# A float32 transformer block on one core: two weight splits moved ahead in the entries, gate and up by turns in the first chunk

## What is computed

```python
def swiglu(x, w_gate, w_up, w_down):
    return (jax.nn.silu(x @ w_gate) * (x @ w_up)) @ w_down
...
        h = layer_norm(DEEPNORM_ALPHA * h + 0.5 * swiglu(h, ffn1_w_gate[l], ffn1_w_up[l], ffn1_w_down[l]),
                       ln1_g[l], ln1_b[l])
        mix = hybrid_mixer(h, w_in[l], q_norm_g[l], kv_norm_g[l], w_uq[l], w_uk[l], w_uv[l], w_q_idx[l],
                           k_idx_ln_g[l], k_idx_ln_b[l], conv_w[l], a_log[l], dt_bias[l], o_norm_g[l], w_out[l])
        h = layer_norm(DEEPNORM_ALPHA * h + mix, ln2_g[l], ln2_b[l])
        h = layer_norm(DEEPNORM_ALPHA * h + 0.5 * swiglu(h, ffn2_w_gate[l], ffn2_w_up[l], ffn2_w_down[l]),
                       ln3_g[l], ln3_b[l])
```

## Time and profile before

| | us |
|---|---|
| median of 3 runs (lowest, highest) | 1978.47 (1975.74, 1982.19) |
| the profiled execution: its own time | 1978.86 |
| its span, first to last instruction | 1977.0 |
| mean granted TensorE clock over it | 0.995 of full speed |

### The profile page before, as it was taken

One profiled execution on the slowest core, in us unless ns is written; L12 is line 12 of the kernel. 1 busy time (PEld: TensorE's weight loads), 2 busy tenths in 40 slices (PEclk: granted clock), 3 DMA queues, 4 the chain that ended last, 5 costly groups with the idle time before them and its releaser, 6 DMA issues.

```text
span 1977.0 us, 28705 instructions
## 1 busy us (share of the span) xinstructions
PE 1948.3 (99%) x10670; PEld 1661.4 (84%) x10670; DVE 1091.0 (55%) x1235; ACT 845.2 (43%) x944; POOL 65.7 (3%) x95
## 2 busy tenths in 40 slices
PE   9999999999999998999999999899999999999997
PEld 7888888888888887999999988788888888888886
DVE  5555545555445465677756757555545555544455
ACT  4444434444434343555645544344444444443332
POOL 0000000000000001300221100000000000000000
PEclk9999999999999999999999999999999999999999
DMA  8666665666566573755532057466666666556663
GB/s 293 190 189 190 191 182 179 190 200 210 190 204 203 193 244 95 223 180 148 142 98 87 22 186 261 131 189 190 189 182 183 193 197 190 186 169 194 208 197 144
DMA packets 185327, 357.30 MB, mean 181 GB/s; under 512 B 11296, under 2 KB 23584, under 8 KB 184240
## 3 DMA queue, kind: packets, MB, share of 16 engines
q1 hardware_dynamic: 183568, 347.43, 56.8%
q0 software_dynamic: 1696, 8.99, 1.4%
HBM read 354.28 MB, written 2.10 MB: 180 GB/s over the span
## 4 chain that ended last, share of the span: by engine, by line
PE 95%; DVE 3%; issue 1%; ACT 1%; DMA 0%; SPq 0%; POOL 0%; POOLq 0%; ACTq 0%; DVEq 0%
PE acc L370 27%; PE acc L372 27%; PE acc L371 27%; PE acc L393 3%; PE acc L397 3%; PE acc L395 3%; PE tp L727 1%; DVE wlo L358 1%; PE acc L1946 1%; PE tp L1959 0%; ACT whi L351 0%; PE acc L1972 0%; PE tp L448 0%; DMA raw<-in_ffn_w_gate_dram 0%; DVE work L1691 0%
## 5 line engine op out<-in xcount | busy, mean ns | idle before, releaser
L358 DVE TENSOR_TENSOR wlo<-raw,whi 128x1024 fp32r<-128x1024 f32 (+2 forms) x637 | 762.4, 1204 | 785.5 <-ACT whi L351 784.6
L351 ACT ACTIVATE whi<-raw 128x1024 fp32r<-128x1024 f32 (+2 forms) x637 | 656.2, 1039 | 943.4 <-PE acc L372 880.8
L370 PE MATMUL acc<-whi,xT 128*128 128x512 f32 (+2 forms) x1652 | 636.3, 385 | 13.6 <-DVE wlo L358 12.8
L372 PE MATMUL acc<-whi,xT 128*128 128x512 f32 (+2 forms) x1652 | 631.3, 382 | 0.0
L371 PE MATMUL acc<-wlo,xT 128*128 128x512 f32 (+2 forms) x1652 | 630.8, 382 | 0.0
L370 PEld LDWEIGHTS acc<-whi,xT 128*128 128x128 f32 x1652 | 311.6, 189 | 79.4 <-DVE wlo L358 12.8
L372 PEld LDWEIGHTS acc<-whi,xT 128*128 128x128 f32 x1652 | 311.6, 189 | 59.8
L371 PEld LDWEIGHTS acc<-wlo,xT 128*128 128x128 f32 x1652 | 311.8, 189 | 56.7
L370 PE MATMUL acc<-whi,hT 128*128 128x512 f32 x656 | 256.3, 391 | 0.0
L372 PE MATMUL acc<-whi,hT 128*128 128x512 f32 x656 | 255.4, 389 | 0.0
L371 PE MATMUL acc<-wlo,hT 128*128 128x512 f32 x656 | 255.4, 389 | 0.0
(11 more groups left out here) (299 smaller groups left out, 1283.7 us busy)
## 6 DMA issues: line engine op xcount, KB each, us to landing
raw<-in_ffn_w_up_dram SPq DMA_DIRECT2D x176, 512.0 KB, 3.7
raw<-in_ffn_w_down_dram SPq DMA_DIRECT2D x176, 512.0 KB, 4.6
raw<-in_ffn_w_gate_dram SPq DMA_DIRECT2D x175, 512.0 KB, 3.8
raw<-in_w_in_dram SPq DMA_DIRECT2D x48, 512.0 KB, 3.8
raw<-in_w_out_dram SPq DMA_DIRECT2D x32, 512.0 KB, 6.6
raw<-in_w_in_dram SPq DMA_DIRECT2D x32, 260.0 KB, 2.8
raw<-in_w_in_dram SPq DMA_DIRECT2D x16, 456.0 KB, 5.3
raw<-in_w_q_idx_dram SPq DMA_DIRECT2D x8, 512.0 KB, 4.2
```

The lines of the kernel that those rows point to most:

```text
L351: act.activation(hi[:, s, :, 0:w], raw[:, r, :, 0:w], ACT.Copy).then_inc(hi_done, 1)
L358: dve.tensor_tensor(lo[:, s, :, 0:w], raw[:, r, :, 0:w], hi[:, s, :, 0:w].bitcast(F32), ALU.subtract).then_inc(lo_done, 1)
L370: pe.matmul(o, hi, w_hi[:, s, k, 0:width], start=first and k == 0, stop=False)
L372: ins = pe.matmul(o, lo, w_hi[:, s, k, 0:width], start=False, stop=last and k == UNIT_KT - 1)
```

## The change

In both entries ACT makes the high parts of units 9 and 10 before the turns of (2, 1) and (3, 0); DVE normalises (3, 1) and splits unit 9 before its turn of (2, 1), and splits unit 10 before its turn of (3, 0); PE does the transposes of (3, 0) ahead of unit 8 and those of (3, 1) ahead of unit 9. In the first chunk of the first FFN the stream's order is gate 0, up 0, gate 1, up 1, then gate 2 to 7 and up 2 to 7 (`FIRST`); the transfers of x come behind units 1, 3, 5 and 7 (`FIRST_X`); ACT and DVE split unit 1 ahead of x tiles 2 and 3; the tanh of gate comes behind split 11 instead of 9.

```diff
--- before.py
+++ after.py
@@ -421,12 +421,20 @@
 
 
 
-        def entry_pe(pe, u):
-
-            if u == 0:
-                pe.wait_ge(sem("xT_lo_first"), 1)
-            else:
-                pe.wait_ge(sem("xT_lo"), u // 2 + 1)
+        FIRST = [(0, 0), (1, 0), (0, 1), (1, 1)] + [(c, k) for c in range(2) for k in range(2, KU)]
+        FIRST_X = {1: 0, 3: 1, 5: 2, 7: 3}
+
+        def first_units_pe(pe):
+
+            for v, (c, k) in enumerate(FIRST):
+                if v == 0:
+                    pe.wait_ge(sem("xT_lo_first"), 1)
+                    first_unit_mm(pe)
+                else:
+                    if k > 0:
+                        pe.wait_ge(sem("xT_lo"), k // 2 + 1)
+                    unit_mm(pe, F1GU, 0, v, (acc0, acc1)[c], (acc0_free, acc1_free)[c], 0, "w", xT, 2 * k, k == 0,
+                            k == KU - 1, acc0a_done if c == 0 else None)
 
 
         def quarter_of(e, q, t):
@@ -497,13 +505,11 @@
             half_unit(6, 1)
             tile_to_xT_pe(pe, e, 2, 1)
             half_unit(7, 1)
+            tile_to_xT_pe(pe, e, 3, 0)
             for half in range(2):
                 half_unit(8, half)
-            tile_to_xT_pe(pe, e, 3, 0)
-            for half in range(2):
-                half_unit(9, half)
             tile_to_xT_pe(pe, e, 3, 1)
-            for v in range(10, 2 * KU):
+            for v in range(9, 2 * KU):
                 for half in range(2):
                     half_unit(v, half)
 
@@ -522,11 +528,11 @@
             split_hi(act, p, 0, 7)
             tile_to_xT_act(act, e, 2, 0)
             split_hi(act, p, 0, 8)
+            split_hi(act, p, 0, 9)
             tile_to_xT_act(act, e, 2, 1)
+            split_hi(act, p, 0, 10)
             tile_to_xT_act(act, e, 3, 0)
-            split_hi(act, p, 0, 9)
             tile_to_xT_act(act, e, 3, 1)
-            split_hi(act, p, 0, 10)
 
         def entry_splits_dve(dve, e, p):
 
@@ -542,12 +548,12 @@
             tile_to_xT_dve(dve, e, 2, 0)
             norm_tile(dve, e - 1, 3, 0)
             split_lo(dve, p, 0, 8)
-            tile_to_xT_dve(dve, e, 2, 1)
             norm_tile(dve, e - 1, 3, 1)
             split_lo(dve, p, 0, 9)
+            tile_to_xT_dve(dve, e, 2, 1)
+            split_lo(dve, p, 0, 10)
             tile_to_xT_dve(dve, e, 3, 0)
             tile_to_xT_dve(dve, e, 3, 1)
-            split_lo(dve, p, 0, 10)
 
         def tp_pair(i):
             return tp[:, 2 * i:2 * i + 2, :].rearrange("p b (k s) -> p (b k) s", k=2)
@@ -561,13 +567,14 @@
             if q == 0:
                 first_hi(act, slice(0, UNIT_KT), sem("x_first"), sem("xT_hi_first"))
                 split_first_hi(act)
+                split_hi(act, F1GU, 0, 1)
                 first_hi(act, slice(UNIT_KT, 4), sem("x_loaded0"), sem("xT_hi"))
                 return
             first_hi(act, slice(4 * q, 4 * q + 4), sem(f"x_loaded{q}"), sem("xT_hi"))
 
         def entry_act(act, u):
 
-            q = {2: 1, 4: 2, 6: 3}.get(u)
+            q = FIRST_X.get(u)
             if q is not None:
                 to_xT_act(act, q)
 
@@ -581,13 +588,14 @@
             if q == 0:
                 first_lo(dve, slice(0, UNIT_KT), sem("xT_hi_first"), 1, sem("xT_lo_first"))
                 split_first_lo(dve)
+                split_lo(dve, F1GU, 0, 1)
                 first_lo(dve, slice(UNIT_KT, 4), sem("xT_hi"), 1, sem("xT_lo"))
                 return
             first_lo(dve, slice(4 * q, 4 * q + 4), sem("xT_hi"), q + 1, sem("xT_lo"))
 
         def entry_dve(dve, u):
 
-            q = {2: 1, 4: 2, 6: 3}.get(u)
+            q = FIRST_X.get(u)
             if q is not None:
                 to_xT_dve(dve, q)
 
@@ -693,21 +701,18 @@
             up_v = w_up.rearrange("(k p) n -> p k n", p=P)
             down_v = w_down.rearrange("(k p) n -> p k n", p=P)
 
-            def gate_up(c, x_between=None):
+            def gate_up(c):
                 for v, view in ((0, gate_v), (KU, up_v)):
                     for u in range(KU):
-                        if x_between and v + u == 0:
-                            load_first(sp, view)
-                        else:
-                            load_unit(sp, GU[f], c, v + u, view[:, 2 * u:2 * u + 2, bass.ds(c * BANK, BANK)])
-                        if x_between and v + u in (0, 2, 4, 6):
-                            x_between((v + u) // 2)
-
-            if f == 0:
-                gate_up(0, load_x)
-            else:
-                for v, (c, k) in enumerate(ENTRY):
+                        load_unit(sp, GU[f], c, v + u, view[:, 2 * u:2 * u + 2, bass.ds(c * BANK, BANK)])
+
+            for v, (c, k) in enumerate((FIRST, ENTRY)[f]):
+                if f == 0 and v == 0:
+                    load_first(sp, gate_v)
+                else:
                     load_unit(sp, GU[f], 0, v, (gate_v, up_v)[c][:, 2 * k:2 * k + 2, 0:BANK])
+                if f == 0 and v in FIRST_X:
+                    load_x(FIRST_X[v])
             with sp.Fori(1, GATE_CHUNKS) as c:
                 gate_up(c)
             if f == 0:
@@ -747,18 +752,16 @@
 
         def ffn_pe(pe, f):
             def gate_up(c, prev):
-                if not prev and f == 1:
-                    entry_units(pe, 2, F2GU)
+                if not prev:
+                    if f == 0:
+                        first_units_pe(pe)
+                    else:
+                        entry_units(pe, 2, F2GU)
                     return
                 for u in range(KU):
-                    if not prev:
-                        entry_pe(pe, u)
-                    if u == 0 and not prev and f == 0:
-                        first_unit_mm(pe)
-                    else:
-                        unit_mm(pe, GU[f], c, u, acc0, acc0_free, c + n0[GU[f]], "w", xT, 2 * u, u == 0, u == KU - 1,
-                                acc0a_done)
-                    if u == 3 and prev:
+                    unit_mm(pe, GU[f], c, u, acc0, acc0_free, c + n0[GU[f]], "w", xT, 2 * u, u == 0, u == KU - 1,
+                            acc0a_done)
+                    if u == 3:
                         hT_pe(pe, f, c)
                 for u in range(KU):
                     unit_mm(pe, GU[f], c, KU + u, acc1, acc1_free, c + n1[GU[f]], "w", xT, 2 * u, u == 0,
@@ -790,7 +793,7 @@
             def gate_up(c, prev):
                 if not prev and f > 0:
                     entry_splits_act(act, 2, GU[f])
-                gate_read = KU + 1 if prev or f == 0 else KU + 5
+                gate_read = KU + 1 if prev else KU + (3, 5)[f]
                 for u in range(LEAD if prev or f == 0 else ENTRY_SPLITS, 2 * KU + LEAD):
                     split_hi(act, GU[f], c, u)
                     if not prev and f == 0:
@@ -2196,8 +2199,6 @@
         @block.scalar
         def _(act):
             to_xT_act(act, 0)
-            for u in range(1, LEAD):
-                split_hi(act, F1GU, 0, u)
             ffn_act(act, 0, False)
             mixer_act(act)
             ffn_act(act, 1, True)
@@ -2205,8 +2206,6 @@
         @block.vector
         def _(dve):
             to_xT_dve(dve, 0)
-            for u in range(1, LEAD):
-                split_lo(dve, F1GU, 0, u)
             ffn_dve(dve, 0, False)
             mixer_dve(dve)
             ffn_dve(dve, 1, True)
```

## The result

The changed kernel takes 1959.89 us (median of four runs, 1959.32 to 1962.30) against 1978.66 us. The ratio is 0.9907, 95% interval 0.9888 to 0.9925. The forecast was 1959.9 us. The profiled execution took 1962.3 us with a span of 1960.5 us, 16.5 less than before, so it is the slowest of the four: where its extra 2.4 us lie is the more instructive part of this case.

What follows compares the result with a forecast made beforehand. PE is busy 99% of the 1977.0 us span, so only its waits and low clock can be won. Gains of 9.0 + 9.2 + 0.8 = 19.0 us off 1978.86 give 1959.9 us, range 1956.5 to 1966.5.

Steps and rivals of the forecast that it cites:

- The entries: Mixer and second FFN entries: new orders remove PE's waits and low clock, 9.0 and 9.2 us.
- The walk through the queues: Mixer's entry, followed engine by engine: splits and turns come in time, so the new orders close the whole stretch.
- The low half of turn (2,1): Entry, VectorE: ends 0.3 us late, at about 762.2, which costs nothing.
- Unit 8's slack: Entry, second half of unit 8: 1.1 us of slack for the turn it waits for; only lateness over that shows.
- Unit 11: Entries: next to be late, since its split must wait until unit 9 is done; priced at 0.
- The first chunk: First FFN's start: second unit's load, ahead of 256 KB of x, lands earlier; 0.8 us, ends 0 and 1.8.
- rival D: First four units: alternating accumulators costs PE its clock, 11 us more, 1971; sign: clock below 1 in first 20 us; chance 0.05.
- B: Entries: the wait moves to unit 11, up to 1 us plus a clock drop up to 3 us, 1964; chance 0.08.
- C: Entries: clock falls without PE waiting, as two transpose groups stand close together; 7 us stay, 1967; chance 0.06.
- E: Entries: turn of (2,1) behind split 9 and its load, so a late landing stops PE in unit 8; 1985; chance 0.02.

Runs made afterwards that it cites:

- e1: Kernel before with only the entries changed, first chunk as before: 1962.36 us, ratio 0.9911.
- e3: Kernel before, old first chunk; ScalarE and VectorE in the new order of the entries, PE in the old one: 1963.24 us, ratio 0.9915.
- e4: Kernel before, old first chunk; PE in the new order of the entries, ScalarE and VectorE in the old one: 1963.21 us, ratio 0.9918.
- e9: Kernel before with eleven small unused matmuls behind the transposes of (3,0) and of (3,1) in both entries: 1973.33 us, ratio 0.9975.
- e2: Kernel before with only the first chunk changed, entries as before: 1977.10 us, ratio 0.9989.
- e5: The changed kernel measured again, unaltered, on one chip with three variants of it: 1960.07 us.
- e6: Changed kernel with six small unused matmuls behind PE's first unit: 1960.38 us.
- e7: Changed kernel with x tiles 2 and 3 loaded ahead of the second unit's weights, as in the kernel before: 1961.31 us.
- e8: Changed kernel with SP waiting for the first x tiles before issuing loads behind the second unit's weights: 1959.03 us, ratio 0.9900 to the kernel before.
- e10: e8 with the split of unit 10 also ahead of the turn of (2,1) on ScalarE and VectorE: 1958.89 us, ratio 0.9897.

## Why the prediction was right, and where it was not

**The entries, 9.0 and 9.1 us.** The forecast was 9.0 and 9.2, from the waits and the low clock behind them, and the runs show both: the waits go when the queues are untied (e1, e3, e4), the low clock when PE is kept busy (e9). Pricing the whole stretch, its actual time less the work in it at full clock, took waits, restarts and low clock in one number, and that is why it came out: the waits alone are 11.1 us. The sum holds for single executions too: 18.1 us less for the entries and 1.4 more or 1.0 less for the start of unit 2 give 1962.2 and 1959.8 us, and the profiled ones took 1962.30 and 1959.95.

**The walk through the queues.** Split 9 was put at 756.6 on the old time scale; it ran at 758.12 on one that is 1.62 us later, so at 756.5. The low half of turn (2,1) was to be 0.3 us later; counted from its transposes it is 0.1 us later (763.63 - 761.56 against 761.90 - 759.94). Unit 8's slack was put at 1.1 us and is 1.3. Unit 11 was named as the next to be late and priced at nothing. It starts 2.51 us after unit 10 in the mixer's entry (769.09, 771.60) and 2.72 in the second FFN's (1247.13, 1249.85), without a gap, and both stretches are within 0.1 us of the sum of their matmuls.

**The first chunk, 0.8 us.** Here the mechanism was right and the size was off, by what was left out. The landing alone did about what was said: with the old order it is at 8.76 to 9.03 us in five profiles (before, e1, e3, e4, e9), with the new one at 8.80, 7.04, 8.02 and 8.05 (changed, e2, e5, e6), on average 0.95 us earlier against 0.8. What the step lacked is that it is not a fixed price. PE's wait behind the first unit lasted 1.65 to 2.6 us with the old order and 0.1 to 2.0 with the new, and where the clock fell, unit 2 came 1.5 to 1.6 us later still. By unit 2's start, 14.22, 15.79, 15.83, 14.30 and 14.05 with the old order (e9 has it too) and 15.61, 12.27 and 13.26 with the new, the first chunk is worth 1.1 us on average, with so few profiles no more than a hint; the median of e2 gives 1.7, and e1's less e5's 2.3, which were measured on different chips. How much the new first chunk is worth stays open between nothing and some 2 us. The Trainium skill (page "DMA: Bandwidth & Descriptors", section "Two DMAs through the same engine are not ordered") says that nothing orders transfers across the engines, by which the place in the queue is worth nothing certain. The landings bear out both halves of that: within one order they vary by up to 1.8 us (7.04 to 8.80), and on average the place is worth 1.0 us. A rule on what is guaranteed is not one on what usually comes first.

**The sign of rival D misled.** The prediction said that a clock below 1 in the first 20 us would show D, the alternation of accumulators. The first profile showed exactly that. But e1 and e3 have the old order and the same low clock, and e2 and e5 the new one at full clock. The sign should have been tied to the wait: PE stood 2.04, 2.3 and 2.6 us ahead of the three low stretches. The Trainium skill (page "TensorE: Matmul & The Clock Gate", section "A second HAM failure mode: psum-queue depth-cycling") tells of a kernel whose clock swung as it cycled through PSUM banks. That does not happen here: e2 and e5 alternate at a granted clock of 1.00.

**B, C and E** did not occur: no wait at unit 11, no low clock in the entries, no stop in unit 8. That the total met the forecast within 0.1 us is partly luck, since the start of unit 2 in the changed first chunk differs by over 3 us between executions (12.27 to 15.61).

## What to carry to other kernels

When one engine starves for work that another has queued behind something the first must do, look at the order of the two queues and not at the amount of work: moving the independent item ahead, in either queue, frees both, and the slack of the item that is pushed back can be read off and used up. Price such a wait over the whole stretch, with the slow matmuls behind it, and expect the spread of the single times to shrink with it. At a cold start, try to hold back the transfers that are not needed yet (worth 1.0 us here).

## What the hardware showed that was not expected

- Standing costs twice, and not the same each time. Behind waits of 2.04, 2.3 and 2.6 us in the first chunk the matmuls went at 1.2 GHz; behind waits of 1.65, 1.9 and, in e7, 2.2 us they did not. In the entry of the second FFN, the same kernel code waits 2.9 us twice in both profiles, and runs 5.6 us at 0.50 behind the second wait in the kernel before and at 1.00 in e2:

```profile
1258.70:1264.60 5.90, 5.85 (x26) 4.86 (x27) 3.49 (x3) 1.77 (x3) 0.00 (x0) 1.00 0.75 240
```

  This is a likely reason for the spread of the single times: 1973.8 to 1982.7 us before, with five long waits; 1972.4 to 1976.3 with those of the entries filled; 1958.9 to 1959.2 with none (e8). The twelve times of e2 fall into two groups, 1973.4 to 1974.2 and 1977.1 to 1979.4, and its profiled execution, with that entry at full clock, is one of the lower. Without a profile of the upper group that is not shown.
- Holding back SP by 1.5 us, from 2.7 to 4.2, made the kernel 1.0 us faster. The transfer ahead landed at 7.31 and 6.99 us with the hold (e8, e10), at 7.04 to 8.80 without. That the transfers run partly side by side can be seen in what had been moved by the landing, in e5 and in e8:

```profile
0.00:8.02 8.02, 6.28 (x26) 5.73 (x27) 1.95 (x3) 3.17 (x5) 0.75 (x7) 1.00 0.69 234
0.00:7.31 7.31, 5.64 (x23) 5.19 (x24) 1.98 (x3) 3.17 (x4) 0.75 (x7) 1.00 0.71 242
```

  That is 1.88 and 1.77 MB, and x tiles 0 and 1 with the first two units are 1.31 MB, so some 0.5 MB of the transfers behind had come already, with the hold or without. Why the hold then makes the landing earlier, and more regular, is not shown.
